# The delta-rule stage of a hybrid decoder layer, rewritten: order, grouping and fill work

## The reference

```python
dec = exp(where(incl, cum[:, None] - cum[None, :], -inf))
a   = where(strict, b[:, None] * (k @ k.T) * dec, 0)
sol = triangular_solve(eye + a, [b * v, b * exp(cum) * k])      # u, w
delta = u - w @ s
o   = ((q @ k.T) * dec) @ delta + (q * exp(cum)) @ s
s   = exp(cum[-1]) * s + (k * exp(cum[-1] - cum)).T @ delta
```

## Time and profile before

| | |
|---|---|
| median of 3 runs | 7351.94 us (7348.95 to 7352.01) |
| profiled execution | 7354.07 us, its span 7352.4 us |
| TensorE busy | 6491.3 us of the span |
| VectorE, ScalarE busy | 3593.1 and 2128.9 us |
| mean granted TensorE clock | 0.92 |

### The profile page before, as it was taken

One profiled execution on the slowest core, in us unless ns is written; L12 is line 12 of the kernel. 1 busy time (PEld: TensorE's weight loads), 2 busy tenths in 40 slices (PEclk: granted clock), 3 DMA queues, 4 the chain that ended last, 5 costly groups with the idle time before them and its releaser, 6 DMA issues. The chain is left out here.

```text
span 7352.4 us, 111812 instructions
## 1 busy us (share of the span) xinstructions
PE 6491.3 (88%) x42878; PEld 6040.7 (82%) x42878; DVE 3593.1 (49%) x6555; ACT 2128.9 (29%) x3108; POOL 0.7 (0%) x6
## 2 busy tenths in 40 slices
PE   7787877797999997999977878777979999979999
PEld 5666666697999997999966666667979999979999
DVE  2332423333778885555423324233337788845554
ACT  2222222322224442222222222223222244422222
POOL 0000000000000000000000000000000000000000
PEclk8888878898999998999988878878989999989999
DMA  2111111222445665444321212102224456654443
GB/s 89 44 52 39 51 49 24 71 81 89 120 114 150 186 186 192 172 176 176 133 76 46 52 38 53 51 19 71 81 92 118 116 148 189 182 195 177 175 173 130
DMA packets 512751, 804.49 MB, mean 109 GB/s; under 512 B 83616, under 2 KB 321184, under 8 KB 494240
## 3 DMA queue, kind: packets, MB, share of 16 engines
q1 hardware_dynamic: 512464, 800.68, 34.6%
HBM read 616.20 MB, written 186.72 MB: 109 GB/s over the span
## 5 line engine op out<-in xcount | busy, mean ns | idle before, releaser
L1462 PE MATMUL ps<-xh,wh 128*128 128x288 f32 x4608 | 1376.3, 299 | 46.5 <-DVE wl L1678 46.5
L1462 PE MATMUL ps<-xl,wh 128*128 128x288 f32 x4608 | 1361.8, 296 | 0.0
L1462 PE MATMUL ps<-xh,wl 128*128 128x288 f32 x4608 | 1357.1, 295 | 0.0
L1878 PE MATMUL ps<-gh,vh 128*128 128x320 f32 (+1 forms) x4096 | 893.9, 300 | 77.7 <-DVE vl L1943 77.7
L160 PE MATMUL ps<-xn,wr 128*128 128x288 f32 x3072 | 843.5, 434 | 74.3 <-PEq L101 49.2
L1462 PEld LDWEIGHTS ps<-xh,wh 128*128 128x128 f32 x4608 | 867.1, 188 | 49.7 <-DVE wl L1678 47.4
L1878 PE MATMUL ps<-gl,vh 128*128 128x320 f32 (+1 forms) x4096 | 883.6, 297 | 0.0
L1878 PE MATMUL ps<-gh,vl 128*128 128x320 f32 (+1 forms) x4096 | 882.9, 297 | 0.0
L1462 PEld LDWEIGHTS ps<-xh,wl 128*128 128x128 f32 x4608 | 868.3, 188 | 0.0
L1462 PEld LDWEIGHTS ps<-xl,wh 128*128 128x128 f32 x4608 | 867.1, 188 | 0.0
L160 PEld LDWEIGHTS ps<-xn,wr 128*128 128x128 f32 x3072 | 619.3, 205 | 278.0 <-issue 76.9
(11 more groups left out here) (350 smaller groups left out, 8890.4 us busy)
## 6 DMA issues: line engine op xcount, KB each, us to landing
raw<-in_u SPq DMA_DIRECT2D x256, 512.0 KB, 4.2
vr<-in_v SPq DMA_DIRECT2D x512, 256.0 KB, 2.6
activated<-go SPq DMA_DIRECT2D x256, 288.0 KB, 4.5
coefficients<-wt SPq DMA_DIRECT2D x36, 2048.0 KB, 9.3
gb<-activated SPq DMA_DIRECT2D x64, 1152.0 KB, 5.9
wb<-coefficients SPq DMA_DIRECT2D x64, 1152.0 KB, 8.4
wr<-in_w_cm SPq DMA_DIRECT2D x104, 512.0 KB, 4.2
wm<-in_w_merge SPq DMA_DIRECT2D x32, 768.0 KB, 4.3
```

Source lines behind the costliest of these rows:

```text
L1462: last = nc.tensor.matmul(out, wp[:, slot, k, :], xp[:, k, cols], start=(k == 0 and wp is T.wh and xp is T.xh), stop=(k == KD - 1 and wp i ...
L1878: last = nc.tensor.matmul(out, vp[:, x % 4, m * P:(m + 1) * P], gp[:, row, col:col + size], start=begins, stop=False, skip_group_check=True)
```

## The change

- `hgrn_stage` loads the convolution history for the next stage.
- The convolution takes k, then q; v's stands behind the first factor. The norms of k are made first. Column sums share bank 5 with the cumulative decays.
- The decay matrix is multiplied by the betas (`bd`) and by the negated first mask (`first`) ahead of the key products; behind them stand one product and one addition for the first factor.
- `boff` has two buffers, so the mask of level r + 1 is made in level r. Each level runs on two groups of tiles, (0, 1) and (2, 3 and 4), with PSUM banks and semaphore counts of their own, and `rt` is updated before `rr`; level 6 leaves `rt` out.
- The fill work becomes 13 blocks, `ahead(0)` to `ahead(12)`: the attention values are three of them (4, 5, 6: tiles in pairs), block 2 is made in two pieces, blocks 3 to 8 stand in levels 1 to 6, and blocks 9 to 11 are dealt out in pieces of two steps through the scan (`feed`).
- v and k are turned in levels 2 to 4 through bank 6; the sample tile's chain stands in level 4 to the scan's tile 0; each prompt tile's output follows its step; the sample states' products follow the output's norm sums.

In the diff a line of dots stands for lines left out, removed ones among them (they are in the listing above). `square_sums`, `scores` and `turn` are the products of the listing's L137, L761 and L771/L776/L799 over the tiles given; `scale` is L926, `convolve` is L914 to L921, `root` is L858; blocks 4 to 6 of `ahead` are L750 over a pair of tiles; `silu_done`, `kss`, `x_ready` and the like keep their meaning.

```diff
             load_tile(sp, T, s, l, h, GDN_W + 2, 2)
             load_tile(sp, T, s, l, h, GDN_W + 3, 3)
             load_sample_state(sp, T, s, l, h, T.d["state_hgrn"])
+            for c in range(3):
+                sp.dma_start(history(T.conv[c])[:, :, 0:3], T.d["conv_in"][l, h, c]).then_inc(s["hist_in"], 16)
...
+        def spare(n):
+            return bank(T, 3 if n in (1, 2) else 6 if n == 12 else 7)[:, 0:HALF]
+        def group(r, a):
+            return range(2) if a == 0 else range(2, TILES if r < 3 else 4)
...
+                load_tile(sp, T, s, l, h + 1, RET_W + 1, 2, after=7)
+                load_tile(sp, T, s, l, h + 1, RET_W + 2, 3, after=9)
...
+            def ahead(n, first=0, count=KD):
...
+                u = n if n < 4 else n - 1
+                c, a = divmod(u, 2)
+                wslot, loads = ATT_SLOTS[c]
+                if first == 0:
+                    if a == 0 and loads:
+                        pe.wait_ge(s["w"][wslot], 16 * loads)
+                    if n == 2:
+                        pe.wait_ge(s["ss_ln"], 2)
+                    elif n > 2 and n != 12:
+                        pe.wait_ge(s["taken"], n)
+                for kk in range(first, first + count):
+                    last = nc.tensor.matmul(spare(n), T.wr[:, wslot, kk, :], T.xn[:, kk, a * HALF:(a + 1) * HALF],
+                                            start=(kk == 0), stop=(kk == KD - 1))
+                if first + count == KD:
+                    last.then_inc(s["ahead"], 1)
...
+            ahead(0)
+            ahead(1)
+            square_sums(0, 1)
...
+            pe.wait_ge(s["taken"], 2)
+            square_sums(1, 0)
...
+            pe.wait_ge(s["btb_ready"], 1)
+            pe.wait_ge(s["taken"], 1)
+            for t in range(TILES):
+                last = nc.tensor.matmul(tile(betab, t), tile(btb, t), T.ident, start=True, stop=True)
+            last.then_inc(s["betab_done"], 1)
+            ahead(2, 0, 4)
+            pe.wait_ge(s["qk_ready"], 1)
+            scores(0, k, range(TILES))
+            ahead(2, 4, 4)
+            pe.wait_ge(s["r1_ready"], 1)
+            pe.wait_ge(s["ec_done"], 1)
+            turn(4, rr, range(TILES), "rt_turned")
...
+            scores(6, q, range(4))
             for r in range(1, LEVELS):
...
+                if r == LEVELS - 1:
+                    pe.wait_ge(s["kss_copied"], 1)
+                    nc.tensor.transpose(bank(T, 6)[:, P:2 * P], kss[:, 0:P], T.ident).then_inc(s["kss_turned"], 1)
                 pe.wait_ge(s["boff_ready"], r)
...
+                for a in range(2):
+                    pe.wait_ge(s["rt_ready"], 2 * r - 1 + a)
+                    for t in group(r, a):
+                        last = nc.tensor.matmul(tile(bank(T, a), t - 2 * a), tile(boff[r % 2], t), tile(rt, t),
+                                                start=True, stop=True)
+                    last.then_inc(s["w_done"], 1)
+                if r < 5 or more:
+                    ahead(r + 2)
                 if r == 1:
+                    pe.wait_ge(s["sc_ready"], 1)
+                    scores(6, q, (4,))
+                if r == 3:
                     pe.wait_ge(s["vt_ready"], 1)
...
+                    turn(6, v, (4,), "turned")
+                if r == 4:
+                    pe.wait_ge(s["keys_ready"], 1)
+                    turn(6, k, (4,), "kt_turned")
+                for a in range(2):
+                    pe.wait_ge(s["w_out"], 2 * r - 1 + a)
+                    if r > 1:
+                        pe.wait_ge(s["rr_ready"], 2 * r - 3 + a)
+                    if r < LEVELS - 1:
+                        for t in group(r, a):
+                            last = nc.tensor.matmul(tile(bank(T, 4 + a), t - 2 * a), tile(rr, t), tile(wz, t),
+                                                    start=True, stop=True)
+                        last.then_inc(s["zt_done"], 1)
+                    for t in group(r, a):
+                        last = nc.tensor.matmul(tile(bank(T, 2 + a), t - 2 * a), tile(wz, t), tile(rr, t),
+                                                start=True, stop=True)
+                    last.then_inc(s["zr_done"], 1)
+                if r == 2:
+                    pe.wait_ge(s["silu_done"], 3)
+                    pe.wait_ge(s["sc_ready"], 2)
+                    turn(6, v, range(4), "turned")
+                if r == 3:
+                    pe.wait_ge(s["vt_ready"], 2)
+                    turn(6, k, range(4), "kt_turned")
+                if r == 4:
+                    pe.wait_ge(s["s_loaded"], 16)
+                    pe.wait_ge(s["keys_ready"], 2)
+                    for b in range(DEC_B):
+                        last = nc.tensor.matmul(bank(T, 6)[:, b * DEC_T:(b + 1) * DEC_T], T.s_in[:, b, :],
+                                                k[:, SEQ + b * DEC_T:SEQ + (b + 1) * DEC_T], start=True, stop=True)
+                    last.then_inc(s["kss_done"], 1)
+            def feed(n, first, count=2):
+                if more:
+                    ahead(n, first, count)
+            def output(t):
+                o = T.ps[:, 4 * BANK + t * P:4 * BANK + (t + 1) * P]
+                nc.tensor.matmul(o, tile(delta, t), tile(T.sc, t), start=True, stop=(t == 0))
+                if t:
+                    nc.tensor.matmul(o, T.st[:, t, :], tile(qe, t), start=False, stop=True)
             for t in range(4):
                 if t:
                     pe.wait_ge(s["st_step"], t)
...
+                    nc.tensor.matmul(bank(T, 0, P), tile(k, t), T.st[:, t, :], start=True, stop=True
+                                     ).then_inc(s["ks_done"], 1)
+                    feed(*((9, 4), (10, 2), (11, 0))[t - 1])
+                    pe.wait_ge(s["x_ready"], t)
+                pe.wait_ge(s["rr_ready"], 2 * LEVELS - 3 + t // 2)
...
+                nc.tensor.matmul(bank(T, 1, P), tile(rr, t), tile(xr if t else bv, t), start=True, stop=True
+                                 ).then_inc(s["delta_done"], 1)
+                if t == 0:
+                    pe.wait_ge(s["xs_ready"], 1)
+                    nc.tensor.matmul(bank(T, 5, P), tile(rr, 4), tile(xr, 4), start=True, stop=True
+                                     ).then_inc(s["sdelta_done"], 1)
+                feed(*((9, 0), (9, 6), (10, 4), (11, 2))[t])
                 pe.wait_ge(s["delta_ready"], t + 1)
...
+                nc.tensor.matmul(step, T.kt[:, t, :], tile(delta, t), start=True, stop=True).then_inc(s["u_done"], 1)
+                output(t)
+                feed(*((9, 2), (10, 0), (10, 6), (11, 4))[t])
+            pe.wait_ge(s["sdelta_ready"], 1)
+            nc.tensor.matmul(bank(T, 5, P), tile(delta, 4), tile(T.sc, 4), start=True, stop=False)
+            for b in range(DEC_B):
+                last = nc.tensor.matmul(bank(T, 5)[:, b * DEC_T:(b + 1) * DEC_T], T.s_in[:, b, :],
+                                        qe[:, SEQ + b * DEC_T:SEQ + (b + 1) * DEC_T], start=False, stop=(b == DEC_B - 1))
+            last.then_inc(s["o_ready"], 1)
+            feed(11, 6)
+            pe_finish(nc, pe, T, s, 0)
             pe_sample_state(nc, pe, T, s)
...
             if more:
...
+                pe.wait_ge(s["st_ready"], 1)
+                ahead(12)
...
+            for i, (c, src) in enumerate(((1, k), (0, q))):
+                silu(i, src)
+                act.wait_ge(s["silu_done"], i + 1)
                 nc.scalar.activation(sq[c][:, 0:N], src[:, 0:N], ACT.Square).then_inc(s["sq_done"], 1)
...
+                take(i)
+            for i, c in enumerate((1, 0)):
+                act.wait_ge(s["ss_done"], i + 1)
+                nc.scalar.activation(two(sq[c]), halves(T, 2 * i), ACT.Ln, bias=T.eps).then_inc(s["ss_ln"], 1)
...
+            root(0, 1)
             act.wait_ge(s["dec_in"], 1)
             nc.scalar.activation(dec, dec, ACT.Exp).then_inc(s["dec_exp"], 1)
+            nc.scalar.activation(ec, bank(T, 4, NP_), ACT.Exp).then_inc(s["ec_done"], 1)
+            root(1, 0)
...
+            take(2)
...
+                for a in range(2):
+                    cols = slice(group(r, a)[0] * P, (group(r, a)[-1] + 1) * P)
+                    act.wait_ge(s["w_done"], 2 * r - 1 + a)
+                    nc.scalar.copy(wz[:, cols], bank(T, a, len(group(r, a)) * P)).then_inc(s["w_out"], 1)
+                if r < 5:
+                    take(r + 2)
+                elif more:
+                    if r == 5:
+                        act.wait_ge(s["conv_out"], 96)
+                    take(r + 2)
...
+                    silu(2, v)
...
+            for t in range(4):
+                if more and t == 3:
+                    take(10)
...
                 if more and t == 1:
                     take(9)
             act_square(nc, act, T, s)
...
+            act_root(nc, act, T, s, 0)
             if more:
                 take(11)
+                take(12)
...
+            for c in range(3):
+                link(nc.vector.memset(xp[c][:, 0:3], 0.0))
+            convolve(1, k)
```

(48 more changed lines are left out.)

283 lines of the change are left out of this document (91 added, 192 removed).

## The result

The kernel with the change takes **6993.68 us** (median of 4 runs, 6992.7 to 6998.46), the kernel before beside it 7351.98 (7348.95 to 7352.02): a ratio of 0.9515, 95% interval 0.9498 to 0.9531. The forecast was 7,018 in a range of 6,975 to 7,120; the change gave 358 us where 334 were forecast. The profiled execution took 6998.46 (span 6996.8), the slowest of the four.

What follows compares the result with a forecast made beforehand. The prediction took the delta-rule stage to be bound by a row of handoffs, no engine saturated. Savings of 6 x 41.8 + 2 x 41.8 = 334 us gave 7,018 us against the median, range 6,975 to 7,120.

Steps and rivals of the forecast that it cites:

- History early, at nothing: Convolution history loaded one stage earlier: costed at nothing, or at 3.1 us per head if that earlier stage's end waited for it.
- Start, 21.1 us: Front of the delta-rule stage: first level starts at 26.6 us instead of 47.7, saving 21.1 us.
- the walk: Step-by-step timing of the changed stage with a successor: it ends at 95.4 us instead of 137.8.
- Levels, 3.7 us: The levels of the stage: 42.8 us instead of 46.5, saving 3.7 us, with more projection work in them.
- The 2 us of waiting forecast between levels 1 and 2: Start of the levels: TensorE waits about 2 us, as the first update starts at 34.1 though its product is there at 32.3.
- Scan and end, 17.6 us: From the end of the inverse to the stage's end: 26.0 us instead of 43.6, saving 17.6 us.
- Last heads: Last head of each layer, without blocks from 7 on: 90.1 us instead of 131.9, saving 41.8 us each.
- the 0.6 added for forgotten handoffs: Whole stage with a successor: 0.6 us added for handoffs missed, giving 96.0 us and a saving of 41.8.
- the clock was held: Denied by a rival: clock stays at its old mean 0.83, or group handoffs cost more; 7,130 us, chance 0.22.
- the sign given, near 1.0 from 8 us on: Sign expected in the changed profile: TensorE's granted clock near 1.0 from 8 us into the stage on.
- Slower, by the clock alone: Rival: TensorE at half clock after the first half projection, 40 us more a stage, some 7,600 us; chance 0.02.
- Saves the start alone: Rival: levels and scan gain nothing, only 21 us a stage saved, 7,184 us; chance 0.06 including up to no change.

## Why the prediction was right, point by point

*History early, at nothing:* right within 0.06 to 0.6 us a head as the change stands. But 3.1 us was the wrong price of the alternative. In the old kernel that wait was not on the path at all: without it the first W product stayed where it was. In the new one, loading it in the stage costs 6 us a head, since the wait grew to 5.6 and half clock stretched what followed.

*Start, 21.1 us:* measured 22.4 in the second head (first W product at 25.3, forecast 26.6). The key products started at 19.1 for 19.75; the walk was about a microsecond slow from there on. In five of the eight stages the first W product came at 26.3 to 26.5, almost the forecast, but for a reason that the forecast did not have: a clock at half for 3.4 us. No single part does it: the history alone left it unchanged, reordering alone made it 0.3 to 1.0 later. Up to the first W product TensorE was busy for 37.4 of 47.7 us before, and for 24.1 of 25.3 now. So 13.3 us of the gain is busy time that left the front, for levels and scan, and 9 is waiting that is gone.

*Levels, 3.7 us:* measured 4.7 (41.8 for 46.5), from the first W product to the last update. The 2 us of waiting forecast between levels 1 and 2 did not occur: the row at 517.27 has 0.30. An update of 256 columns took 0.42, as assumed. The group split costs nothing visible, as argued, and saves 0.9 us a stage or more.

*Scan and end, 17.6 us:* measured 17.6 (25.9 for 43.5). Tiles are 4.0 to 4.1 us apart (forecast 3.95), the sample outputs, the sum and the issue each 2 us before their forecast times, which is what start and levels brought. What ends the stage was forecast as the sample state's DMA: in stages with a successor it was about even with the last block (landing at 577.04, the block's copy until 576.98), and moving it forward brought nothing there.

*Last heads:* the mis-sized term. The forecast was 90.1 us with the DMA's landing, on the assumption that the clock falls in the bare scan. Counted likewise, up to 4.24 us (the gap where no landing is waited for) ahead of the next stage, they took 83.5 and 87.4 us for 132.4 and 132.5. The inverse was done after 61.2 and 61.0 us (forecast 62.8). In the first of the two the clock held until 1100 us, 74 us into the stage, and tiles were 2.77 us apart; in the second, with the same instructions, it fell after 67 us, and that is the 4 us between them. So 48.9 and 45.0 came where twice 41.8 were forecast: 10 of the 24 us by which the result beats the forecast, and some 4 of them are luck with the clock. The rest is 2.5 us in each of six stages (44.3 for 41.8). The forecast had 89 us of work and 6 of waiting; in the second head TensorE was busy for 90.6 and idle for 2.4. What was not needed is the 0.6 added for forgotten handoffs, the 2 us of waiting in level 2, and the quicker front, with a little given back in gaps.

*Rivals:* the clock was held in the levels and the scan of every stage with a successor; the sign given, near 1.0 from 8 us on, held in three of the eight stages, and in the other five but for 3.4 us in the front (in the last heads until the scan or the finish). The Trainium skill ("TensorE: Matmul & The Clock Gate", the section on psum-queue depth-cycling) warns of short idles between groups of products. Several of 0.3 to 0.8 us did no harm where work was dense; in bare stretches of a last head they did. The clock alone is worth 110 of 358 us in the old order; it is neither nothing nor the whole. "Slower, by the clock alone" needed a mean under 0.65; the lowest of a stage is 0.84. "Saves the start alone" fails by the levels' and the end's 22 us.

*Slips in the working,* none of which moves the forecast: blocks 3 to 8 hold three half projections and the values, not four halves; 40 us more in each of eight stages would be some 7,670 us, not 7,600; and levels 5 and 6 of a last head are said to take 8 us where the walk's own figures, 57.0 and 62.8, leave 5.8, which is what they took.

Still open: in which of two ways the clock goes. For the front the traces show a sign. Nine kernels here (the change and all its variants but the one with the history loaded in the stage) do the same in their first 16 us. In their 72 stages the clock first rises 5.1 to 6.2 us after the start. In the 30 where it rose at 5.62 us or before it stayed up; in the 42 where it rose at 5.65 or later it fell again at 16 us. The outcome thus goes with the time at which the clock rose. What sets that time, and whether it also decides the later falls, no run here shows. Not taken out one by one were the order of the three convolutions, the product that level 6 leaves out, and the sample tile's earlier chain; their share of the gain is not known.

## What to carry to other kernels

When a stage is a chain of handoffs, list the work of the busiest engine that nothing waits for, and deal it out in pieces no longer than the handoffs they cover; a lump covers one and leaves the rest bare, and moving it within the chain only moves the wait. Where products behind a wait run at half clock, price a new wait on the path at up to twice its length. Judge parts of such a change by taking them out of the finished version: in the old one two of them left the front as long as it was, out of the new one each cost 12 to 59 us, and these prices (183 us together) don't add up to the gain.

## What the runs showed of the hardware

A wait costs more than itself: 1.7 us more in front of the first factor became 3 us a stage, 5.6 us at the start of VectorE's work 6 to 8, whole blocks in the scan 5 there and 5 behind it. Each time the trace shows products at half clock behind the wait.

Stages of the same work, with the same idle time (26.7 and 27.0 us), took 137.6 and 133.9 us, TensorE's clock 0.83 and 0.86. An edit that left the first W product where it was thus made the kernel 16 us faster. The two last heads of the change, with the same instructions, took 81.4 and 85.3 us, and in the run with whole blocks in the scan, whose last heads are unchanged, 81.4 both. Differences of up to 16 us between two versions of this kernel say nothing about their edits unless the stage in question shows them.

The fall of the clock in the front went with the time at which it had risen: it fell again in none of the 30 stages in which it rose at 5.62 us or before, and in all of the 42 in which it rose at 5.65 us or later.

Products that nobody reads, put in gaps, made the old kernel 1.5% faster and a bare last head 6 us shorter (81.5 for 87.7).
